# Sparse attention with values stationary: row sums folded into the turning product, outputs leaving PSUM already turned

## The reference

```python
# per head h (16 heads, 64 wide), for every token t; keys s <= t that were chosen
logits = q[t, h] @ k[s, h] + rel_bias[bucket(t - s), h]
p      = softmax(logits over the chosen s)
o[t,h] = sum_s p[s] * v[s, h]          # (512, 16, 64)
# then o.reshape(512, 1024) @ dsa_w_o, the residual, a layer norm, the feed-forward
```

## Time and profile before

| | |
|---|---|
| median of three runs | 3969.64 us (3968.69 to 3972.82) |
| the profiled execution | 3975.83 us, of which its span is 3974.1 us |
| PE busy over the span | 3641.0 us (92%) |
| PEld busy | 2988.0 us (75%) |
| DVE busy | 2327.4 us (59%) |
| ACT busy | 1485.5 us (37%) |
| POOL busy | 1331.0 us (33%) |
| first to last start of L3469 | 3368.3 to 3507.7 us |
| mean granted TensorE clock | 0.942 of full speed |

### The profile page before, as it was taken

The page is one execution under the profiler, slowest core; times in us unless marked ns, Lnnn a source line. Parts: engine busy times, 40 slices in busy tenths (PEclk is TensorE's granted clock), DMA queues, the critical chain, the costliest instruction groups (busy, mean ns, idle before and its releaser), DMA issues. The chain is left out here.

```text
span 3974.1 us, 60891 instructions
## 1 busy us (share of the span) xinstructions
PE 3641.0 (92%) x23405; PEld 2988.0 (75%) x23405; DVE 2327.4 (59%) x3603; ACT 1485.5 (37%) x2431; POOL 1331.0 (33%) x831
## 2 busy tenths in 40 slices
PE   7999979898988999799996997997799978889998
PEld 7878857688988999688885344995688854678887
DVE  1932148425999887688885664336566324755652
ACT  2311336334446994333332232121255303334540
POOL 1724400334875335332221001233234521322453
PEclk9999989899999999899998998998899988598999
DMA  5724320535768889999996343001433336023331
GB/s 191 254 85 135 107 98 1 211 110 178 238 220 289 317 314 362 341 363 353 353 354 211 90 125 131 30 30 45 129 85 95 116 116 104 1 97 95 94 108 63
DMA packets 377759, 659.69 MB, mean 166 GB/s; under 512 B 24488, under 2 KB 236200, under 8 KB 374356
## 3 DMA queue, kind: packets, MB, share of 16 engines
q1 hardware_dynamic: 331692, 483.43, 37.7%
q0 software_dynamic: 36864, 134.23, 9.0%
q10 hardware_dynamic: 9000, 39.21, 2.5%
HBM read 556.60 MB, written 100.19 MB: 165 GB/s over the span
## 5 line engine op out<-in xcount | busy, mean ns | idle before, releaser
L93 PE MATMUL ex_hb<-wb_x_hi,ex_uh 128*128 128x384 f32 x1024 | 351.2, 343 | 22.6 <-POOL ex_ul L1740 22.6
L2311 POOL TENSOR_TENSOR pf_wl<-pf_raw,pf_wh 128x2048 fp32r<-128x2048 f32 x48 | 221.1, 4608 | 392.2 <-ACT pf_wh L2258 392.2
L94 PE MATMUL ex_hb<-wb_x_lo,ex_uh 128*128 128x384 f32 x1024 | 345.3, 337 | 0.0
L95 PE MATMUL ex_hb<-wb_x_hi,ex_ul 128*128 128x384 f32 x1024 | 345.0, 337 | 0.0
L93 PE MATMUL es_ob<-es_vh,es_ah 128*128 128x512 f32 x768 | 299.6, 390 | 24.1 <-DVE es_al L2031 24.1
L93 PE MATMUL pf_acc<-wb_x_hi,pf_wh 128*128 128x512 f32 (+2 forms) x768 | 301.8, 393 | 4.7 <-DVE wb_x_lo L2353 4.7
L94 PE MATMUL pf_acc<-wb_x_lo,pf_wh 128*128 128x512 f32 (+2 forms) x768 | 301.6, 393 | 0.0
L95 PE MATMUL pf_acc<-wb_x_hi,pf_wl 128*128 128x512 f32 (+2 forms) x768 | 301.4, 392 | 0.0
L94 PE MATMUL es_ob<-es_vl,es_ah 128*128 128x512 f32 x768 | 299.2, 390 | 0.0
L95 PE MATMUL es_ob<-es_vh,es_al 128*128 128x512 f32 x768 | 299.2, 390 | 0.0
L2013 POOL DMA_INDIRECT es_near<-in_peer_v,wb_picked x128 | 150.3, 1174 | 383.5 <-DVE wb_po L2034 360.7
(11 more groups left out here) (509 smaller groups left out, 9359.5 us busy)
## 6 DMA issues: line engine op xcount, KB each, us to landing
ex_u<-in_uT SPq DMA_DIRECT2D x128, 512.0 KB
es_v<-in_peer_v SPq DMA_DIRECT2D x32, 2048.0 KB
pf_raw<-in_w_up SPq DMA_DIRECT2D x88, 512.0 KB, 5.0
ip_raw<-in_w_in SPq DMA_DIRECT2D x112, 256.0 KB, 4.3
scratch_act<-ex_ge SPq DMA_DIRECT2D x128, 192.0 KB
scratch_G<-eg_gates ACTq DMA_DIRECT2D x12, 2048.0 KB
es_ge<-scratch_act SPq DMA_DIRECT2D x32, 768.0 KB
es_g<-scratch_G SPq DMA_DIRECT2D x32, 768.0 KB
```

The source lines that it names most:

```text
L93: pe.matmul(out, left[0], right[0], start=start, stop=False)
L94: pe.matmul(out, left[0], right[1], start=False, stop=False)
L95: return pe.matmul(out, left[1], right[0], start=False, stop=stop)
L2311: pool.tensor_tensor(wl[:, u], raw[:, u], wh[:, u].bitcast(F32), ALU.subtract).then_inc(w_lo, 1)
```

## The change

Three things change in the loop.

- The reciprocal of the row sum is taken right after the exponentials (`spread_sum`), and DVE multiplies the identity with it into a diagonal matrix `sa_dg` of 128 x 128. The turning step is no longer a transpose but a full fp32 product of the exponentials with this diagonal matrix, which turns and scales at once.
- The product with the values has the values stationary (64 columns) and the turned exponentials moving (128 columns). Its output has features on partitions; an even head writes partitions 0 to 63 and the following odd head partitions 64 to 127 of the same buffer of `sa_op`. So a buffer holds a pair p of heads, and pair p of tile i is exactly chunk p mod 8 of the transposed output.
- ACT writes the high part of each pair (`upper`) and DVE the low part (`lower`) inside the loop, both from PSUM. The transposes of `sa_rows` after the loop, and `sa_rows` itself, are gone. Product m, for even m from 4 on, waits until `lower(m / 2 - 2)` has read the buffer (the wait on `o_out`).

```diff
                     if TURN <= n < N + TURN:
                         m = n - TURN
-                        pe.wait_ge(exp_done, m + 1)
+                        pe.wait_ge(spread, m + 1)
                         if m >= 2:
                             pe.wait_ge(p_copied, m - 1)
                         for c in range(m // AH + 1):
-                            mm = pe.transpose(tp[:, m % 2, c * P:(c + 1) * P], e[:, m % SL, c * P:(c + 1) * P], ident[:])
+                            mm = pe.matmul(tp[:, m % 2, c * P:(c + 1) * P], e[:, m % SL, c * P:(c + 1) * P], dg[:, m % SL, :],
+                                           start=True, stop=True)
                         mm.then_inc(p_turned, 1)
                     if n >= PV:
                         m = n - PV
                         h, i = job(m)
                         pe.wait_ge(p_copied, m + 1)
-                        if m >= 2:
-                            pe.wait_ge(o_scaled, m - 1)
+                        p = m // 2
+                        if m % 2 == 0 and p >= 2:
+                            pe.wait_ge(o_out, p - 1)
                         for c in range(i + 1):
-                            mm = pe.matmul(op[:, m % 2, 0:64], eT[:, m % SL, c * P:(c + 1) * P],
-                                           o["v"][:, c, h * 64:(h + 1) * 64], start=(c == 0), stop=(c == i))
+                            mm = pe.matmul(op[half(h), p % 2, 0:P], o["v"][:, c, h * 64:(h + 1) * 64],
+                                           eT[:, m % SL, c * P:(c + 1) * P], start=(c == 0), stop=(c == i))
                         mm.then_inc(o_done, 1)
-                pe.wait_ge(o_scaled, N)
-                for i in range(TT):
...
+                def spread_sum(m):
+
+                    dve.wait_ge(exp_done, m + 1)
+                    if m >= SL:
+                        dve.wait_ge(p_turned, m - SL + 1)
+                    dve.reciprocal(rs[:, m:m + 1], st[:, m, 1:2]).then_inc(inverted, 1)
+                    dve.wait_ge(inverted, m + 1)
+                    dve.tensor_scalar(dg[:, m % SL, :], ident[:], rs[:, m:m + 1], None, ALU.mult).then_inc(spread, 1)
+
+                def lower(p):
+
+                    k, at = placed(p)
+                    dve.wait_ge(hi_done, p + 1)
+                    dve.tensor_tensor(split[1][:, k, at], op[:, p % 2, 0:P], split[0][:, k, at].bitcast(F32),
+                                      ALU.subtract).then_inc(o_out, 1)
+
                 for n in range(0, N, 2):
                     k, i = job(n)
                     logits(n)
                     find(i + 1, k)
                     logits(n + 1)
                     take(i + 1, k)
-                    if n >= PV + 1:
-                        scale_o(n - PV - 1)
+                    if n:
+                        spread_sum(n - 2)
                     find(i + 1, k + 1)
-                    if n >= PV:
-                        scale_o(n - PV)
+                    if n:
+                        spread_sum(n - 1)
                     take(i + 1, k + 1)
+                    if n >= 8:
+                        lower((n - 8) // 2)
...
+                def upper(p):
+
+                    k, at = placed(p)
+                    act.wait_ge(o_done, 2 * p + 2)
+                    act.activation(split[0][:, k, at], op[:, p % 2, 0:P], ACT.Copy).then_inc(hi_done, 1)
...
+                    if n >= 6 and n % 2 == 0:
+                        upper((n - 6) // 2)
```

More of the change, by code:

```diff
@@ L3379, in sparse_attention @@
     with phase(nc, "bias_loaded", "ident_loaded", "index_done", "relu_done", "scored", "cleared", "causal", "chosen", "masked",
-               "bias_ready", "s_done", "logits_done", "exp_done", "p_turned", "p_copied", "o_done", "o_scaled", "o_turned",
-               "hi_done", "o_out", "dve_steps") as (
+               "bias_ready", "s_done", "logits_done", "exp_done", "inverted", "spread", "p_turned", "p_copied", "o_done",
+               "hi_done", "o_out") as (
             bias_loaded, ident_loaded, index_done, relu_done, scored, cleared, causal, chosen, masked,
-            bias_ready, s_done, logits_done, exp_done, p_turned, p_copied, o_done, o_scaled, o_turned,
-            hi_done, o_out, dve_steps), ExitStack() as ctx:
+            bias_ready, s_done, logits_done, exp_done, inverted, spread, p_turned, p_copied, o_done,
+            hi_done, o_out), ExitStack() as ctx:
         sb, ps = tensors(nc, ctx)
@@ L3396, in sparse_attention @@
         rs = sb("sa_rs", [P, N])
-        rows = sb("sa_rows", [P, TT, D])
+        dg = sb("sa_dg", [P, SL, P])
         sp_ = ps("sa_sp", [P, 4, T])
@@ L3400, in sparse_attention, with half, placed @@
         op = ps("sa_op", [P, 2, T])
-        rp = sp_[:].rearrange("p u t -> p (u t)").rearrange("p (u k t) -> p u k t", u=2, k=KD)
+        def half(h):
+            return slice(64 * (h % 2), 64 * (h % 2) + 64)
+        def placed(p):
+            return p % (AH // 2), slice(p // (AH // 2) * P, p // (AH // 2) * P + P)
         with nc.Block() as block:
@@ L3465, in _ @@
                         pe.wait_ge(p_copied, m + 1)
-                        if m >= 2:
-                            pe.wait_ge(o_scaled, m - 1)
+                        p = m // 2
+                        if m % 2 == 0 and p >= 2:
+                            pe.wait_ge(o_out, p - 1)
                         for c in range(i + 1):
-                            mm = pe.matmul(op[:, m % 2, 0:64], eT[:, m % SL, c * P:(c + 1) * P],
-                                           o["v"][:, c, h * 64:(h + 1) * 64], start=(c == 0), stop=(c == i))
+                            mm = pe.matmul(op[half(h), p % 2, 0:P], o["v"][:, c, h * 64:(h + 1) * 64],
+                                           eT[:, m % SL, c * P:(c + 1) * P], start=(c == 0), stop=(c == i))
                         mm.then_inc(o_done, 1)
-                pe.wait_ge(o_scaled, N)
-                for i in range(TT):
[L3474 to L3478, removed]
             @block.vector
             def _(dve):
-                step = Steps(dve, dve_steps)
                 for n, (i, h) in enumerate(index):
@@ L3517, in logits @@
                                              3.0e38, ALU.add, ALU.min, st[:, n, 0:1]).then_inc(logits_done, 1)
[L3519 to L3525, removed]
+                def spread_sum(m):
[10 more added lines that the diff above has]
+                                      ALU.subtract).then_inc(o_out, 1)
+                dve.wait_ge(ident_loaded, 16)
                 for n in range(0, N, 2):
@@ L3542, in _ @@
                                           ALU.mult).then_inc(masked, 1)
[L3543 to L3546, removed]
+                spread_sum(N - 2)
+                spread_sum(N - 1)
+                for p in range((N - 8) // 2, N // 2):
+                    lower(p)
             @block.scalar
@@ L3568, in _ @@
                                        accum_out=st[:, n, 1:2]).then_inc(exp_done, 1)
-                for i in range(TT):
-                    act.wait_ge(o_turned, i + 1)
-                    act.activation(split[0][:, :, i * P:(i + 1) * P], rp[:, i % 2], ACT.Copy).then_inc(hi_done, 1)
+                    if n >= 6 and n % 2 == 0:
+                        upper((n - 6) // 2)
+                for p in range((N + TURN - 6 + 1) // 2, N // 2):
+                    upper(p)
 def sparse_block(nc, d, split):
```

## The result

The changed kernel takes 4081.43 us (median of 4 runs, 4079.93 to 4083.48); before took 3969.16 us (4 runs on the same chip, 3966.94 to 3972.82). The ratio is 1.0282, 95% interval 1.0264 to 1.0300: 112 us slower. The forecast was 4040 with a range of 4002 to 4082. The direction is right, and the time stands within 1 us of the upper edge of the range, outside the forecast's own 4025 to 4060; the size of the change was forecast at 70 us and came out at 112.

What follows compares the result with a forecast made beforehand. A DVE-PE loop through a buffer of `sa_op`, released mid-pair, bounds the stage. With the new wait for `lower` the tiles and end sum to +83.6 us, less 13.9 for the clock: +70 on 3969.6 gives 4040 us, range 4002 to 4082.

Steps and rivals of the forecast that it cites:

- The wait: PE's every second value product waits for `lower`, ending DVE's pair; turns of 5.43, 7.93, 10.45 and 6.61 us by tile.
- The bursts at low clock: Three PE bursts per turn (product, turn, product) at low clock: 1.45, 2.74 and 4.03 us in tiles 0, 1 and 2.
- The step that failed: tile 3: Last tile: scaling the identity on DVE adds 0 us a pair, PE's clock stays up; seven turns cost +16.9 us.
- The clock credit: PE's clock rises late in bursts: -10.3 us in tile 2 and -3.6 in tile 1, -13.9 together.
- The end: From the last logits to the last `lower`: 13.0 us against 16.3 before, -3.3 us.
- Low clock in tile 3 too: Rival: PE's clock is low in tile 3 as well, turn 9.95 us, +115 us, 4084 us; chance 12%.
- Full clock throughout: Rival: PE's new dense bursts run at full clock in all tiles, +44 us, 4014 us; chance 22%.
- the wait is not the last: Rival: `lower` does not end DVE's pair, only turn n-2 joins the loop, +25 us, 3995 us; chance 7%.
- Not slower: Rival: the wait is not the last and PE's clock rises, -5 us, 3965 us; chance 4%.

Runs made afterwards that it cites:

- experiment 1: The changed kernel with `lower` moved from the end of DVE's pair to ahead of the logits: 3976.81 us, ratio 1.0018 to the kernel before.
- experiment 2: The changed kernel with one more wait on POOL in tile 3, so its addition does not run beside `spread_sum`: 4058.06 us, ratio 1.0215.
- experiment 3: The changed kernel with unused identity products on PE behind turn n-3, filling the gap where PE waits: 4039.49 us, ratio 1.0177.
- experiment 6: The changed kernel with `lower` and both `spread_sum` calls ahead of the logits: 3962.09 us, ratio 0.9985 to the kernel before.
- experiment 7: The kernel before with both `scale_o` calls ahead of the logits: 3950.26 us, ratio 0.9957.
- experiment 5: The kernel before with a full fp32 product with the identity as its turn instead of a transpose: 3970.00 us, ratio 1.0005.

## Why the prediction was right, and which term was mis-sized

**The wait: right.** The prediction named `lower` at the end of DVE's pair as what every second value product waits for. The waits and the pair above show it, and experiment 1 takes 105 of 112 us away by moving it. The mean turns of tiles 1 and 2 were forecast at 7.65 and 10.18 us (61.2 and 81.4 by 8) and measured at 8.01 and 10.31.

**The bursts at low clock: too low.** Where the bursts and the scores of a turn all ran at low clock, it took 8.36 us in tile 1 (logits at 3415.26 and 3423.62) for 7.93, and 10.97 in tile 2 (3484.56 and 3495.53) for 10.45; in tile 0 it took 5.85 for 5.43. So each such turn cost 0.4 to 0.5 us more than forecast. In tile 2 that is the three bursts: in the pair shown they start 1.45, 1.58 and 1.47 us apart, 4.50 together for 4.03. Each takes 0.16 to 0.29 us beyond its three chunks of 0.43, which I had put in once for all three. Tile 0 came 2.5 us over its term, tile 1 2.9 and tile 2 1.1; that tile 2 came out so close is in part luck, since the scores gave back what the bursts took: 1.20 us from scores to logits in the pair shown for 1.68, because they ran with the clock already rising.

**The step that failed: tile 3.** The prediction said of the scaling of the identity "between -0.1 and 0 us a pair; I take 0", from rows of the same operation with nothing on POOL beside it, and of tile 3 "the gap is only about 1.5 us at full clock, so it should stay up". It measured 0.70 and 1.11 us, some 1.2 us a pair, the gap became 2.8 us, and the clock 0.79. Tile 3 grew by 38.0 us and not by 16.9; with POOL's addition kept away (experiment 2) its seven turns take 45.8 us where 45.1 were forecast. So 20 of the 21 us are this one term: 1.3 us a turn by itself and 1.6 through the clock (experiment 3). The old scaling read `sa_op` in PSUM and ran beside the same additions; all of it in tile 3 of the kernel before:

```profile
L3524 DVE TENSOR_SCALAR sa_rows<-sa_op,sa_rs x14: 282/284/286, 3474.1 to 3498.1; 128x64 f32<-128x64 f32 x14
```

One pair of it starts at 3477.86 and 3478.25, while POOL's additions run from 3477.22 to 3479.72, and takes 0.28 and 0.29 us. The exchange of a PSUM operand for an SBUF one was in the diff, and I priced only its columns. Experiment 2 shows that POOL's additions lengthen the new scaling; that the old one was spared because of its operand in PSUM is not shown by itself, since it also had 64 columns and not 128.

The Trainium skill has both halves of this: on the page SBUF — State Buffer, SBUF: two separate sides, DVE and GpSimd share a pair of ports that one of them holds for a whole instruction when DVE's instruction is of the form that uses two read ports, and on VectorE: DVE Perf Modes, Why PSUM operands drop a tier, an operand in PSUM rules that form out. The trace agrees, though it does not show the form of an instruction: both scalings end 0.1 us behind the end of a POOL instruction (3558.81 + 0.71 = 3559.52 and 3559.62 + 1.11 = 3560.73; POOL's two, of 1.24 to 1.26 us, at about 3559.43 and at 3560.65), and in experiment 2 they take 286 ns.

**The clock credit: wrong.** -13.9 us was credited to tiles 1 and 2 for a clock that rises late in a burst. It does rise (0.61 and 0.69), but most of what had it lies off the loop. In tile 2 the scores gained, so that the turn fell from 10.97 to 10.30; in tile 1 a burst now and then (0.62 us for 1.09 at 3443.71, in a turn of 7.79 for 8.36). This did no more than cover the bursts priced too low. Experiment 3 shows what it is worth when it covers the loop: 42 us. The full-clock turns of the prediction were right there, 6.37 and 8.05 measured for 6.11 and 7.88.

The sum closes: +69.7 forecast, 2.5 + 2.9 + 1.1 of loop (bursts less what the clock gave back), 13.9 of credit, 21.1 of tile 3 and 0.4 of the end make 111.6.

**The end: right.** 13.0 us to the last `lower` were forecast; it ends at 3626.92, 13.5 behind the logits at 3613.47.

```profile
3613.47 0.69 DVE L3517 CUSTOM_DVE_ANT_0 sa_lg<-sa_sp,sa_bm 128x512 f32<-128x512 f32 x1 [5.96 <-PE sa_sp L3459]
...
3626.63 0.29 DVE L3533 TENSOR_TENSOR wb_x_lo<-sa_op,wb_x_hi 128x128 fp32r<-128x128 f32 x1 [0.99 <-ACT wb_x_hi L3572]
3627.70 0.10 POOL L2317 MEMSET pf_mhalf<- 128x1 f32 x1 [20.48 <-POOLq L44]
```

**The rivals.** "Low clock in tile 3 too" gave 4084 and a turn of 9.95; 4081 and 9.46 were measured. That is the number, and half of its mechanism: the clock did fall in tile 3, but because the scaling held DVE up, and it was up at the end, where the rival had 8 us. That the time lies inside the range at all is luck: the range reached so far only to take in this rival's neighbourhood, and the cause was another. "Full clock throughout" (4014) and "the wait is not the last" (3995) did not come; experiment 1, in which the wait is not the last, is at 3977, lower than priced because the clock then rises. "Not slower" had two conditions, the wait not the last and a rising clock. Experiment 1 meets both and stands at 3977, not at the rival's 3965: tile 1 is no shorter than before (36.8 us for 36.3) where the rival had 6 us less. Only with the scalings moved as well (experiment 6) does the kernel come to 3962.

## What to carry to other kernels

A buffer's release that is the last instruction of one engine's loop body, waited for by the other engine's next one, makes the two take turns; put the releases first in the body and price that before the arithmetic, and then give the old kernel the same order before comparing: here experiment 6 is 6 us below the kernel before, but 12 above experiment 7. An operand that moves from PSUM to SBUF on DVE has to be checked for what POOL does at the same time. A clock that rises is worth something only for the instructions that lie on the loop.

## What was unexpected of the hardware

- A DVE `TENSOR_SCALAR` of 128 columns, SBUF to SBUF, takes 0.29 us alone and 0.70 to 1.12 us beside a POOL `TENSOR_TENSOR` of 1.24 us; the one of 64 columns with its source in PSUM stays at 0.28.
- In tile 2 before, PE shows 44 of 47 us busy at a clock of 0.50 through the whole tile. With full products for the turn it shows 31 of 38 at 0.96 (experiment 5), and with DVE's scalings first and the transposes kept, 33 of 38 at 0.73 (experiment 7). No run here separates what the chip counts; that stays open.
- A value product with 64 stationary and 128 moving columns costs 0.5 us a chunk in a burst of three at low clock (1.51 for six records), the same as with the two exchanged: which of the two operands stands still did not matter to PE.
